# A hybrid decoder layer in split float32: three of four gated sums turned by 32x32 squares and a DRAM round trip, and five moved steps around them

## The reference, cut to what matters

```python
def token_mixer(h, w_in, conv_dw, conv_db, conv_ln_g, conv_ln_b, w_conv_out, w_attn_out, w_out):
    z = h @ w_in                                  # 2048 -> 12288 columns
    q, k, v, u, ga, gc = jnp.split(z, ...)
    o = moba_attention(to_heads(q), to_heads(k), to_heads(v))   # 256 rows: one causal block, ALiBi, 16 heads of 128
    y_attn = o... @ w_attn_out                    # 2048 x 2048
    y_conv = conformer_conv(u, ...)               # depthwise 31 taps, norm, silu, @ w_conv_out (1024 x 2048)
    merged = jax.nn.sigmoid(ga) * y_attn + jax.nn.sigmoid(gc) * y_conv
    return merged @ w_out                         # 2048 x 2048
```

## Time and profile before

| what | value |
|---|---|
| median of 3 runs | 2112.12 us (2111.99 to 2113.73) |
| the profiled execution's own time | 2111.3 us |
| its span, first to last instruction | 2109.5 us |
| PE busy | 2095.7 us of the span |
| DVE busy | 1877.2 us |
| ACT busy | 1402.9 us |

### The profile page before, as it was taken

How to read it: one execution, slowest core, us unless ns; L and a number is a source line. 1 busy time by engine, 2 the same in 40 slices (tenths; PEclk the granted TensorE clock), 3 DMA queues, 4 the chain that set the end, 5 groups by cost and what they waited for, 6 DMA issues and landing times.

```text
span 2109.5 us, 23778 instructions
## 1 busy us (share of the span) xinstructions
PE 2095.7 (99%) x9386; PEld 1734.6 (82%) x9386; DVE 1877.2 (89%) x1420; ACT 1402.9 (67%) x1313; POOL 216.7 (10%) x345
## 2 busy tenths in 40 slices
PE   9999999999999999999999999999999999999998
PEld 7888888888888888888888888888888888888886
DVE  7899999999996889999999986659899999999996
ACT  6677777777775546766676445335677777777773
POOL 0111111101110001011100000000111111100110
PEclk9999999999999999999999999999999999999999
DMA  9798988888985759998898556755788988899892
GB/s 369 253 295 260 279 270 266 291 300 277 289 279 231 276 158 311 299 269 270 304 301 262 212 185 240 260 178 200 244 294 255 282 272 267 290 302 278 288 285 113
DMA packets 92397, 556.65 MB, mean 264 GB/s; under 512 B 13056, under 2 KB 13440, under 8 KB 35200
## 3 DMA queue, kind: packets, MB, share of 16 engines
q1 hardware_dynamic: 68544, 437.69, 54.7%
q0 software_dynamic: 23744, 117.46, 25.8%
HBM read 534.13 MB, written 20.97 MB: 263 GB/s over the span
## 4 chain that ended last, share of the span: by engine, by line
PE 88%; DVE 8%; DMA 2%; ACT 1%; issue 1%; SPq 0%; DVEq 0%; ACTq 0%
PE acc L2259 14%; PE acc L2261 14%; PE acc L2260 14%; PE tb L2259 12%; PE tb L2261 12%; PE tb L2260 12%; PE acc L2197 3%; PE acc L2199 3%; PE acc L2198 3%; DVE g_lo L1338 3%; DVE cacc L1777 3%; DMA g_raw<-in_groups 1%; PE tb L2245 1%; DVE w_lo L1315 1%; DVE g_raw L1346 1%
## 5 line engine op out<-in xcount | busy, mean ns | idle before, releaser
L1338 DVE TENSOR_TENSOR g_lo<-g_raw,g_hi 128x2048 fp32r<-128x2048 f32 x506 | 1147.6, 2286 | 120.4 <-ACT g_hi L817 119.8
L817 ACT ACTIVATE g_hi<-g_raw 128x2048 fp32r<-128x2048 f32 x506 | 964.4, 1916 | 319.8 <-DVE g_raw L1346 121.5
L2259 PE MATMUL acc<-g_hi,xF_hi 128*128 128x512 f32 x1184 | 464.3, 392 | 0.6 <-ACT acc L899 0.6
L2261 PE MATMUL acc<-g_hi,xF_lo 128*128 128x512 f32 x1184 | 461.1, 389 | 0.0
L2260 PE MATMUL acc<-g_lo,xF_hi 128*128 128x512 f32 x1184 | 460.7, 389 | 0.0
L2259 PE MATMUL tb<-g_hi,xF_hi 128*128 128x512 f32 x760 | 296.3, 390 | 0.3 <-DVE g_lo L1338 0.2
L2261 PE MATMUL tb<-g_hi,xF_lo 128*128 128x512 f32 x760 | 295.7, 389 | 0.0
L2260 PE MATMUL tb<-g_lo,xF_hi 128*128 128x512 f32 x760 | 295.7, 389 | 0.0
L1346 DVE TENSOR_TENSOR g_raw<-g_raw,g_raw 128x2048 f32<-128x2048 f32 x120 | 274.3, 2286 | 1.3
L2259 PEld LDWEIGHTS acc<-g_hi,xF_hi 128*128 128x128 f32 x1184 | 222.3, 188 | 46.8 <-ACT acc L899 1.0
L2261 PEld LDWEIGHTS acc<-g_hi,xF_lo 128*128 128x128 f32 x1184 | 222.2, 188 | 46.8
(11 more groups left out here) (180 smaller groups left out, 2307.7 us busy)
## 6 DMA issues: line engine op xcount, KB each, us to landing
g_raw<-in_groups SPq DMA_DIRECT2D x356, 1024.0 KB, 7.2
g_raw<-in_groups POOLq DMA_DIRECT2D x80, 1024.0 KB, 8.6
raw<-in_stream SPq DMA_DIRECT2D x80, 512.0 KB, 4.5
bounce<-h_sq POOLq DMA_DIRECT2D x40, 256.0 KB, 5.5
h_in<-bounce POOLq DMA_DIRECT2D x160, 64.0 KB, 2.6
ln_gb<-in_ln SPq DMA_DIRECT2D x6, 1024.0 KB, 6.6
g_raw<-in_groups SPq DMA_DIRECT2D x6, 512.0 KB, 9.7
res<-in_x_rows SPq DMA_DIRECT2D x1, 2048.0 KB, 16.6
```

What stands on the lines that cost most here:

```text
L817: act.activation(g_hi[:, n % RING], source[:], ACT.Copy).then_inc(g_hi_ready, 1)
L1338: dve.tensor_tensor(g_lo[:, n % RING], source[:], f32(g_hi[:, n % RING]), ALU.subtract).then_inc(g_lo_ready, 1)
L2259: pe.matmul(bank, x_hi_ap, g_hi[:, n % RING, blk], start=begin, stop=False, skip_group_check=True)
L2261: return pe.matmul(bank, x_lo_ap, g_hi[:, n % RING, blk], start=False, stop=end, skip_group_check=True)
```

## The change

The sums of chunks 0, 1 and 2 of the convolution product are no longer transposed by PE. DVE transposes them in 32x32 squares into a buffer `m_sq` (`merge_squared`), POOL writes that to DRAM (`m_bounce`, one DMA of 512 KB) and reads it back in four DMAs of 128 KB that put the squares in their places, ACT and DVE make the parts from there. PE still transposes the fourth. The multiplication of the fourth chunk is done tile by tile between the low parts of `mix_out`'s units (`conv_row`), and the first chunk of `mix_out` now waits for one sum before unit 0 and, before unit 2, for the count `b_merge + TT * MERGED`, which is that of three sums. Beside it: `scores` stands one product group later in each half on PE; the queries' write to DRAM is issued ahead of the keys' read; maxima and negation are taken by pair of heads; `normalised` and the second `exponents` stand ahead of piece `Q3`; in block 0 the bank copy stands ahead of the split of `P6b`; the first tile of attention chunk 1 is gated after unit 2 of chunk 2 instead of after unit 3.

```diff
@@ ACT
-                split_sum(f, g, "P6b", "qb", "T2b")
                 if g:
+                    split_sum(f, g, "P6b", "qb", "T2b")
                     act.wait_ge(v_out, 2 * g)
                 else:
                     act.wait_ge(acc_out[1], 4)
                 fork(f, g, acc[:, BZ], acc[:, BW], "P5b")
+                if not g:
+                    split_sum(f, g, "P6b", "qb", "T2b")
...
-                split_loaded(f, g, "Q3", "Q3")
                 if heads:
                     exponents(g - 1, 1)
+                split_loaded(f, g, "Q3", "Q3")
...
-            hi(conv_out, 0, *range(12))
+            hi(conv_out, 0, *range(16))
             merged_hi(0)
-            hi(conv_out, 0, 12, 13, 14, 15)
+            hi(mix_out, 0, 0, 1)
             merged_hi(1)
-            hi(mix_out, 0, 0, 1, 2, 3)
+            hi(mix_out, 0, 2, 3, 4, 5)
             merged_hi(2)
-            hi(mix_out, 0, 4, 5, 6, 7)
+            hi(mix_out, 0, 6, 7)
             merged_hi(3)
@@ DVE
                 lo_group(f, g, "P3a", "ua")
+                lo_group(f, g, "P6b", "qb")
                 if heads:
                     biased_scores(g - 1, 0)
-                lo_group(f, g, "P6b", "qb")
+                    maxima(g - 1, 0)
+                lo_group(f, g, "P3b", "ub")
                 if heads:
                     biased_scores(g - 1, 1)
-                    maxima(g - 1)
-                lo_group(f, g, "P3b", "ub")
+                    maxima(g - 1, 1)
...
-                lo_group(f, g, "Q3", "Q3")
                 if heads:
                     normalised(g - 1)
+                lo_group(f, g, "Q3", "Q3")
...
                 lo(attn_out, 2, j)
+                if j == 2:
+                    attn_rows(2, (0,))
                 taps(3)
-            attn_rows(2)
+            attn_rows(2, (1,))
...
+            def merge_squared(c):
+                for t in range(TT):
+                    dve.wait_ge(merged, 2 * c + t + 1)
+                    dve.transpose(m_sq[c][:, :, t].rearrange("p c b n -> p b c n"),
+                                  sig_a[:, c, t].rearrange("p (b c n) -> p b c n", b=BLK, c=QD)).then_inc(m_squared, 1)
@@ POOL
                     squares_out(g - 1, k_squared, kT[:], k_bounce, k_sent)
+                    squares_out(g - 1, q_squared, q_sq[:], q_bounce, q_sent)
                     heads_in(g - 1, k_sent, kT[:], k_bounce, kT_loaded)
-                    squares_out(g - 1, q_squared, q_sq[:], q_bounce, q_sent)
                     heads_in(g - 1, q_sent, q_sq[:], q_bounce, q_loaded)
...
+            for c in range(MERGED):
+                pool.wait_ge(m_squared, TT * (c + 1))
+                pool.dma_start(m_bounce[c]..., m_sq[c][:]...).then_inc(m_sent[c], 16)
+                pool.wait_ge(m_sent[c], 16)
+                for s in range(QD):
+                    pool.dma_start(m_sq[c][STEP * s:STEP * (s + 1)]..., m_bounce[c, :, :, s]...).then_inc(m_loaded[c], 16)
@@ PE
                 product_group(f, g, "P5a", W, S1, 0, begin=True)
+                product_group(f, g, "P5b", W, S1, 1)
                 if heads:
                     scores(g - 1, 0)
-                product_group(f, g, "P5b", W, S1, 1)
                 wait_fork(f, g, 0)
                 product_group(f, g, "P6a", X, S2, 0)
+                wait_fork(f, g, 1)
+                product_group(f, g, "P3a", Z, S4, 0)
                 if heads:
                     scores(g - 1, 1)
-                wait_fork(f, g, 1)
-                product_group(f, g, "P3a", Z, S4, 0)
...
-                      after={(3, 0): lambda: turn_merged(c - 1)} if c else {})
+                      after={(3, 0): lambda: turn_merged(c - 1)} if c > MERGED else {})
-            chunk(mix_out, 0, 0, UD, 0, oT_parts, u0_mix, groups=groups_of(UD)[:1], ready={(0, 0): wait_lhs(b_merge + 4)},
+            chunk(mix_out, 0, 0, UD, 0, oT_parts, u0_mix, groups=groups_of(UD)[:1],
+                  ready={(0, 0): wait_lhs(b_merge + TT), (2, 0): wait_lhs(b_merge + TT * MERGED)},
                   after={(3, 0): lambda: turn_merged(ND - 1)})
```

More of the change, by code:

```diff
@@ L100 @@
 GATES = len(GATE_CHUNKS)
+MERGED = 3
 LAST_COLS = (slice(0, 2 * COLS), slice(2 * COLS, 3 * COLS), slice(3 * COLS, D))
@@ L303, in build @@
     q_bounce = nc.dram_tensor("q_bounce", (QD, STEP, QD, TT, BLK, STEP), F32, kind="Internal").ap()
+    m_bounce = nc.dram_tensor("m_bounce", (MERGED, QD, STEP, QD, TT, BLK, STEP), F32, kind="Internal").ap()
     kept = nc.dram_tensor("kept", (P, TT, D), F32, kind="Internal").ap()
@@ L406, in build @@
         ct = place("ct", [P, TT, CC], at=raw_F_at)
+        m_sq = [place(f"m_sq{c}", [P, QD, TT, BLK, STEP], at=at) for c, at in enumerate((act_at, c_at - 4 * GW, act_at))]
         cgb = place("cgb", [P, 2, CC], at=raw_F_at + 4 * TT * CC)
@@ L495, in build @@
         stored = sem("stored")
+        m_squared = sem("m_squared")
+        m_sent = [sem(f"m_sent{c}") for c in range(MERGED)]
+        m_loaded = [sem(f"m_loaded{c}") for c in range(MERGED)]
         u_gates = 2
@@ L517, in build @@
         t_merge = t_convt + 4
-        t_ln2 = t_merge + 2 * ND
+        t_ln2 = t_merge + TT * (ND - MERGED)
         def lo_count(n):
@@ L1111, in exponents @@
             def exponents(g, pair):
-                act.wait_ge(smax_ready, 3 * g + 3)
+                act.wait_ge(smax_ready, 6 * g + 3 * pair + 3)
                 for h in (2 * pair, 2 * pair + 1):
@@ L1276, in merged_hi @@
             def merged_hi(c):
+                if c < MERGED:
+                    act.wait_ge(m_loaded[c], 16 * QD)
                 for t in range(TT):
-                    block_hi(oT_hi[:, BLK * c:BLK * (c + 1), t * P:(t + 1) * P], 2 * (c % 2) + t,
-                             t_merge + 2 * c + t + 1)
-            hi(conv_out, 0, *range(12))
+                    if c < MERGED:
+                        act.activation(in_steps(oT_hi, c, t), m_sq[c][:, :, t], ACT.Copy).then_inc(lhs_hi, 1)
+                    else:
+                        block_hi(oT_hi[:, BLK * c:BLK * (c + 1), t * P:(t + 1) * P], 2 * (c % 2) + t,
+                                 t_merge + TT * (c - MERGED) + t + 1)
+            hi(conv_out, 0, *range(16))
             merged_hi(0)
-            hi(conv_out, 0, 12, 13, 14, 15)
+            hi(mix_out, 0, 0, 1)
             merged_hi(1)
-            hi(mix_out, 0, 0, 1, 2, 3)
+            hi(mix_out, 0, 2, 3, 4, 5)
             merged_hi(2)
-            hi(mix_out, 0, 4, 5, 6, 7)
+            hi(mix_out, 0, 6, 7)
             merged_hi(3)
@@ L1788, in biased_scores, with maxima @@
                                              in1=tb[:, h % 2, 0:SC], op0=ALU.mult, op1=ALU.add).then_inc(s_ready, 1)
[L1790 to L1796, removed]
+            def maxima(g, pair):
+                two = slice(2 * pair, 2 * pair + 2)
+                by_half = [m[:].rearrange("p (q h) -> p q h", q=2)[:, :, two] for m in (nmax, smax)]
+                dve.wait_ge(s_ready, HG * g + 2 * pair + 2)
+                for q, cols in enumerate((slice(0, P), slice(P, SC))):
+                    dve.tensor_reduce(by_half[1][:, q], pr[:, two, cols], AX_X, ALU.max).then_inc(smax_ready, 1)
+                dve.wait_ge(smax_ready, 6 * g + 3 * pair + 2)
+                dve.tensor_scalar(by_half[0], by_half[1], -SCALE, None, ALU.mult).then_inc(smax_ready, 1)
             def normalised(g):
@@ L2021, in merged_lo @@
                     blocks, rows = slice(BLK * c, BLK * (c + 1)), slice(t * P, (t + 1) * P)
-                    block_lo(oT_lo[:, blocks, rows], oT_hi[:, blocks, rows], 2 * (c % 2) + t,
-                              b_merge + 2 * c + t + 1)
+                    if c < MERGED:
+                        dve.wait_ge(lhs_hi, b_merge + 2 * c + t + 1)
+                        dve.tensor_tensor(in_steps(oT_lo, c, t), m_sq[c][:, :, t], f32(in_steps(oT_hi, c, t)),
+                                          ALU.subtract).then_inc(lhs_lo, 1)
+                    else:
+                        block_lo(oT_lo[:, blocks, rows], oT_hi[:, blocks, rows], 2 * (c % 2) + t,
+                                 b_merge + 2 * c + t + 1)
             lo(conv_out, 0, 0, 1, 2, 3)
@@ L2028, in _ @@
             merge(0)
+            merge_squared(0)
             lo(conv_out, 0, 8, 9, 10, 11)
+            merge(1)
+            merge_squared(1)
+            lo(conv_out, 0, 12, 13, 14, 15)
             merged_lo(0)
-            merge(1)
-            lo(conv_out, 0, 12, 13, 14, 15)
+            merge(2)
+            merge_squared(2)
+            lo(mix_out, 0, 0, 1)
             merged_lo(1)
-            merge(2)
-            lo(mix_out, 0, 0, 1, 2, 3)
+            conv_row(3, 0)
+            lo(mix_out, 0, 2, 3)
+            conv_row(3, 1)
+            gated_sum(3)
+            lo(mix_out, 0, 4, 5)
             merged_lo(2)
-            merge(3)
-            lo(mix_out, 0, 4, 5, 6, 7)
+            lo(mix_out, 0, 6, 7)
             merged_lo(3)
@@ L2184, in _ @@
                     store_heads(g - 1)
-            for n in range(2, 6):
```

(13 more changed lines are left out.)

12 lines of the change are left out of this document (8 added, 4 removed).

## The result

| | before | changed |
|---|---|---|
| median of 22 runs each | 2112.32 us (2110.38 to 2114.35) | 2116.45 us (2113.43 to 2121.21) |
| ratio, 95% interval | | 1.0018 [1.0012, 1.0023] |
| span of the profiled execution | 2109.5 us | 2114.3 us |

The change makes the kernel slower: the ratio puts it at +3.8 us, between 2.5 and 4.9. The forecast was 2110.1 us with a range up to 2113.8, so the time lies outside it, and for "slower", by over 0.2%, I had given a chance of 0.05. In this document a run's gain or loss is the difference of its median to that of the kernel before on the same chip; by its medians the changed kernel stands at +4.1. The interval of an experiment's ratio is some 0.0009 to each side, 1.9 us, so a difference of less than 2 us between two runs is read from the traces and not shown by the medians.

What follows compares the result with a forecast made beforehand. PE, busy 99% of the span, was taken to bound the kernel. Gains of 5.1 us less a new wait of 3.0 gave -2.1, from the median 2112.12 a forecast of 2110.1 us; range 2107.0 to 2113.8.

Steps and rivals of the forecast that it cites:

- The gains: On PE: transposes 2.6, bank copy 0.25, block 2 scores 0.95 and second weight transposes 0.34, gated row 0.94; 5.1 us leave.
- the new wait: Unit 2 of `mix_out`: PE waits for DVE's low parts of the third sum, 3.0 us including 0.11 behind it.
- the third trip: Third sum's way through DRAM before `mix_out`: 9.0 us taken, 11.4 allowed, no extra cost; bounds 0 and 4.6.
- the multiplication starts at M + 0.20: DVE's fourth-chunk multiplication starts 0.20 us after M, the start of `mix_out`; used to time the third sum's low parts.
- The first two sums have trips that end before DVE turns to them: Before `mix_out`: the first two sums' DRAM trips are in time for DVE, with margins of 3 and 1 us.
- The bank copy: Block 0, PE's `P3a`: the copy moved ahead gains 0.25 us, bounds 0.2 and 0.88; DVE's low part is late next.
- Forecast as worked out, clock kept: 0.46: Main case: the summed forecast of 2110.1 us with PE's clock staying up through the wait at unit 2; chance 0.46.
- The rival: PE's clock falls in the wait at unit 2 of `mix_out`: 2.0 us more, time 2112.1; chance 0.24.
- POOL's and ACT's swaps are hidden by these margins too: Blocks 1 to 4: the reordering on POOL and ACT costs PE 0; bounds 0 and 2 us.
- The margins: Blocks 1 to 4: DVE's low parts are ready ahead of PE by 1.2 us at `P7a` and 0.8 at `Q3`.
- the write is issued about 1.5 us earlier: Block 2 scores: POOL's earlier queries' write and `P5b` ahead both cover PE's 0.79 us wait; gain 0.95.
- DVE falls behind in the blocks: Rival: the 0.8 us margin at `Q3` is used up and 0.5 lost in each of four blocks: 2112.1 us; chance 0.07.

Runs made afterwards that it cites:

- e7: The changed kernel with 4 matmuls, whose results nobody reads, in front of the wait of unit 2 of `mix_out`: 2115.44 us, run once.
- e9: The changed kernel with 8 matmuls, whose results nobody reads, in front of the wait of unit 2 of `mix_out`: 2115.46 us, run once.
- e8: The changed kernel with two sums asked for at unit 2 and ACT's high part of `P3a` ahead of the queries' copy, POOL's order as changed: 2105.82 us.
- e2: The changed kernel with POOL's order of before in the mixing blocks, the keys' four reads ahead of the queries' write: 2112.07 us, ratio 0.9996.
- e4: The changed kernel with two sums asked for at unit 2 and POOL's order of before: 2106.43 us, ratio 0.9971.
- e5: e4 with ACT's high part of `P3a` moved ahead of the queries' copy in the mixing blocks: 2106.05 us, ratio 0.9974.

## Why the prediction was wrong, step by step

*Right.* The gains, 5.1 by the sum: the rows give 5.0, and with both new losses repaired the kernel is 5.9 below before. Also right: the new wait's place, releaser and the engine that bounds it, and that the third trip is in time (10.6 us from the end of the squares; the sum had 9.0, and 11.4 were allowed).

*Mis-sized.* The new wait, 3.0, is 3.5: the term "the multiplication starts at M + 0.20" took DVE's idle of before for granted, and DVE was still at the low parts of units 2 and 3 (0.4 us). Behind it stands a margin that was not there: "The first two sums have trips that end before DVE turns to them". The second took 14.3 us, and DVE waited 1.86 for it; in every trace with the squares it waited, 1.7 to 3.6 us. The bank copy, 0.25, is 0.13; what bounds it is DVE's low part, as said.

*Wrong, first step: "Forecast as worked out, clock kept: 0.46".* The clock fell. I set an idle of 2.8 beside one of 2.7 that was "enough" at the end of the trace, and still held the fall for less likely, on the strength of idles of 0.6 to 0.8. e7 and e9 show no fall behind 1.27 us of idle and a fall behind 2.48. The rival priced it at 2.0; it was 1.6.

*Wrong, second step: "POOL's and ACT's swaps are hidden by these margins too".* The margins, 1.2 at `P7a` and 0.8 at `Q3`, were those of a DVE that is never held, and e8 shows just these. But I had counted them from DVE's bias on and asked only what DVE does. The swap on POOL holds the keys' reads behind the queries' squares. I took "the write is issued about 1.5 us earlier" for an earlier arrival. The write went out 1.2 us earlier in block 2 (900.95 for 902.19), but in block 3 at 969.10, where it had been 968.58: POOL waits for the queries' squares. The reads were issued 3.0 us earlier in block 3 and landed 2.1 us later. ACT waits for them with `P3a` behind, so a margin of 1.2 met a delay of 2.1, and PE paid 0.9. That was 4.4 us (e2, give or take 2; 4.5 by the rows) for which the sum had 0, bounds 0 and 2. The rival "DVE falls behind in the blocks" named the effect, but `Q3` as the place and DVE's work as the cause, and at a chance of 0.07.

The sum with what was measured in place of the failed terms: -2.1 + 0.1 (bank copy) + 0.5 (wait) + 1.6 (clock) + 4.4 (blocks) = +4.5, against +4.1 and +3.8 measured. The clock alone would have left the time in the range; the blocks alone put it outside.

*Open.* Why the queries' reads are slower is argued from the DMA share and not shown by a run. That block 2 keeps a wait at `P7a` in e4 is read from its trace: ACT waits 6.07 us for the queries and copies them at 916.42, DVE waits 4.40 and starts `P3a` at 919.40; in e5 ACT waits 0.68 there and DVE has no idle ahead of `P3a`. No run holds block 2 apart. What part the move of the scores on PE has in the thin margins was not tried by itself.

## What to carry to other kernels

A wait that asks for more than its consumer reads costs what the engine in front still has in its list: check each count against the operands used, and an idle of over 2 us on PE should be priced with the clock's fall unless a trace says otherwise (here the earliest fall came 2.1 us after the last matmul). When a queue's list is reordered, an earlier issue is not an earlier landing: ask what the moved wait now holds back, how full the DMAs are when the held transfers run, and what stands behind the consumer on its in-order engine. The cheapest cure was to put work that needs nothing late ahead of the instruction that waits.

## What the runs showed that I had not expected

The same 512 KB trip, reordered by one position on POOL, took 6.5 instead of 2.9 us for its reads. And PE's clock fell with an idle of 2.48 us and stayed at full level with one of 1.27, each after some 270 us without idle time in PE's row; in the changed kernel it stood at 1.00 through all of the 3.23 us of idle, and 3.7 us nearly all at the lower level followed once PE had started again.
